# Moving four of layer 1's modulation vectors between layer 0's output columns, an earlier score pair, and weight blocks that wait for their own rows

## What is computed

```
for i in range(DEPTH):                                   # DEPTH = 2
    mod = silu_c @ ada_w[i] + ada_b[i]
    mod_c = silu_cc @ ada_w[i] + ada_b[i]
    sh1, sc1, g1, sh2, sc2, g2 = jnp.split(mod[:, None, :], 6, axis=-1)
    h_lat = modulate(rmsnorm(x, norm1_g[i]), sh1, sc1)    # h_ctx alike
    y_lat, y_ctx = even_mixer(...) if i % 2 == 0 else odd_mixer(...)
    x = x + g1 * y_lat
    h2 = modulate(rmsnorm(x, norm2_g[i]), sh2, sc2)
    out = peer(tokens, p_w_q[i], p_keys1[i], p_keys2[i], p_u[i], p_v[i])
    x = x + g2 * out
return rmsnorm(x, final_g)
```

## Time and profile before

| | before |
|---|---|
| median of 3 runs | 2415.6 us (2414.28 to 2417.3) |
| the profiled execution's own time | 2415.03 us |
| its span | 2413.2 us |
| PE, DVE, ACT, POOL busy | 57%, 64%, 15%, 62% |
| moved by DMA | 936.90 MB, mean 388 GB/s |
| queue of the gathers | 84.1% of 16 engines' span |
| queue of SP (weights) | 129.78 MB, 14.6% |

### The profile page before, as it was taken

The page is one execution under the profiler, slowest core; times in us unless marked ns, Lnnn a source line. Parts: engine busy times, 40 slices in busy tenths (PEclk is TensorE's granted clock), DMA queues, the critical chain, the costliest instruction groups (busy, mean ns, idle before and its releaser), DMA issues.

```text
span 2413.2 us, 21643 instructions
## 1 busy us (share of the span) xinstructions
PE 1386.2 (57%) x6926; PEld 621.5 (26%) x6926; DVE 1542.4 (64%) x4025; ACT 360.2 (15%) x731; POOL 1490.2 (62%) x1546
## 2 busy tenths in 40 slices
PE   6997774456674655335443556648866565334333
PEld 2456421123331433001100112315533133001000
DVE  1338578878955665777766655623898646777543
ACT  1421201112301110110100101202222011000000
POOL 0004576677677666767777767630577776777772
PEclk9999886668797877567655766879987787665567
DMA  9967899999999999999999999989999999999997
GB/s 367 346 220 302 323 406 407 409 409 409 382 406 408 405 407 407 410 409 409 409 409 409 405 409 409 406 326 379 353 409 396 404 407 407 409 409 409 410 409 302
DMA packets 286799, 936.90 MB, mean 388 GB/s; under 512 B 27728, under 2 KB 28512, under 8 KB 286432
## 3 DMA queue, kind: packets, MB, share of 16 engines
q0 software_dynamic: 221184, 805.40, 84.1%
q1 hardware_dynamic: 64704, 129.78, 14.6%
q10 hardware_dynamic: 800, 0.34, 0.1%
HBM read 934.36 MB, written 1.05 MB: 388 GB/s over the span
## 4 chain that ended last, share of the span: by engine, by line
DMA 35%; POOL 23%; PE 17%; DVE 12%; issue 10%; ACT 2%; SPq 1%; POOLq 0%; DVEq 0%; ACTq 0%
DMA RING<-in_p_v,IDV 19%; POOL RING L879 16%; DMA RING<-in_p_u,IDX 10%; PE acc L1552 5%; DVE RING L960 4%; POOL WR L879 3%; PE wk L1801 2%; PE wk L1627 2%; PE wk L1841 2%; DMA BC<-in_p_v,IDV 2%; POOL H L879 2%; DMA X<-in_p_v,IDV 2%; POOL BC L879 2%; POOL X L879 1%; PE wk L1583 1%
## 5 line engine op out<-in xcount | busy, mean ns | idle before, releaser
L1552 PE MATMUL acc<-RING,ST 128*32 128x512 f32 x2044 | 569.8, 919 | 522.6 <-DMA RING<-in_p_v,IDV 411.6
L960 DVE SCALAR_TENSOR_TENSOR RING<-RING,acc 128x1024 f32<-128x1024 f32 x576 | 687.4, 1219 | 277.7 <-DMA RING<-in_p_u,IDX 258.6
L879 POOL DMA_INDIRECT RING<-in_p_u,IDX x576 | 558.7, 970 | 412.9 <-DVE IDX L1279 192.6
L879 POOL DMA_INDIRECT RING<-in_p_v,IDV x511 | 496.8, 972 | 218.6 <-issue 144.9
L1552 PEld LDWEIGHTS acc<-RING,ST 128*32 128x32 f32 x2044 | 104.5, 144 | 750.4 <-issue 743.0
L1552 PE MATMUL acc<-WR,ST 128*32 128x512 f32 x428 | 158.7, 935 | 63.8 <-DMA BC<-in_p_v,IDV 53.2
L1552 PE MATMUL acc<-X,ST 128*32 128x512 f32 x288 | 114.4, 911 | 92.3 <-DMA RING<-in_p_v,IDV 92.3
L879 POOL DMA_INDIRECT H<-in_p_u,IDX x82 | 78.9, 962 | 123.5 <-DVE IDX L1279 96.7
L960 DVE SCALAR_TENSOR_TENSOR H<-H,acc 128x1024 f32<-128x1024 f32 x82 | 100.0, 1220 | 81.6 <-DMA H<-in_p_u,IDX 80.3
L879 POOL DMA_INDIRECT WR<-in_p_v,IDV x107 | 101.0, 944 | 32.6 <-issue 31.4
L1552 PE MATMUL acc<-BC,ST 128*32 128x512 f32 x148 | 76.7, 958 | 72.9 <-DMA RING<-in_p_v,IDV 72.9
(11 more groups left out here) (277 smaller groups left out, 2469.7 us busy)
## 6 DMA issues: line engine op xcount, KB each, us to landing
RING<-in_ada_w SPq DMA_DIRECT2D x30, 1024.0 KB, 12.3
WR<-in_p_w_q SPq DMA_DIRECT2D x20, 1024.0 KB, 12.5
WR<-in_ada_w SPq DMA_DIRECT2D x15, 1024.0 KB, 12.8
RING<-in_p_u,IDX POOLq DMA_INDIRECT x576, 17.6
WR<-in_o_w_in SPq DMA_DIRECT2D x9, 1024.0 KB
WR<-in_e_w_in SPq DMA_DIRECT2D x8, 1024.0 KB, 15.0
RING<-in_p_v,IDV POOLq DMA_INDIRECT x511, 18.2
RING<-in_p_w_q SPq DMA_DIRECT2D x7, 1024.0 KB, 6.9
```

Source lines behind the costliest of these rows:

```text
L879: pool.indirect_dma_start(out=row_at(row), out_offset=None, in_=tables[kind], in_offset=bass.IndirectOffsetOnAxis(ap=rows, axis=0)).then_i ...
L960: nc.vector.scalar_tensor_tensor(out=row_at(row), in0=row_at(row), scalar=1.0, in1=acc[:, 1, :], op0=ALU.mult, op1=ALU.mult, accum_out=A[: ...
L1552: ins = nc.tensor.matmul(acc[32 * g:32 * g + 32, 0, hf * 512:hf * 512 + 512], ST[:, c % 2, s, :], row_at(rows[g][0])[:, hf * 512:hf * 512 ...
```

## The change

Three things. In `front0`, layer 1's `ada` 6 (with `adaT`, `adaD`) now stands around layer 0's second output column, and its `ada` 8 behind that column; both leave `front1`. In `fills0`, the context tokens' last score item, heads 6 and 7, stands at fill 2 and not 3. In `block_slots` (moved below `gather_rows`, since it now reads `ROWS`) the ring slots are taken between the layers in the order in which their rows are summed, a block waits for the last sum of its own two rows (`last_sum`) and not for all 512, and the first-layer slots 3, 4, 5 are open to fewer blocks.

```
-    s += [("out", 0, first, 0), ("outD", 0, first, 0), ("out", 0, first, 1), ("ada", 0, 10, 2), ("outD", 0, first, 1), ...
+    s += [("out", 0, first, 0), ("outD", 0, first, 0), ("ada", 1, 6, 2), ("out", 0, first, 1), ("adaT", 1, 6, 2), ("adaD", 1, 6, 2), ("ada", 1, 8, 2), ("adaT", 1, 8, 2), ("adaD", 1, 8, 2), ("ada", 0, 10, 2), ("outD", 0, first, 1), ...
...
-        put(f, 3, ("score", 0, ctx, (6, 7)))
+        put(f, 2, ("score", 0, ctx, (6, 7)))
...
-    s += [("restA", 0), ..., ("restE", 1), ("ada", 1, 6, 2),
+    s += [("restA", 0), ..., ("restE", 1),
...
-    s += [("out", 1, first, 0), ("adaT", 1, 6, 2), ("outD", 1, first, 0), ("out", 1, first, 1), ("adaD", 1, 6, 2), ("outD", 1, first, 1),
-          ("normA", 1, 2, 0), ("ada", 1, 8, 2), ("normB", 1, 2, 0), ("hT", 1, 2, first), ("adaT", 1, 8, 2), ("adaD", 1, 8, 2)]
+    s += [("out", 1, first, 0), ("outD", 1, first, 0), ("out", 1, first, 1), ("outD", 1, first, 1),
+          ("normA", 1, 2, 0), ("normB", 1, 2, 0), ("hT", 1, 2, first)]
...
+def last_sum(slot):
+    rows = [("x", 2), ("x", 3)] if slot == YSLOT else [("ring", 2 * RSLOTS.index(slot) + i) for i in range(2)]
+    return max([i + 1 for i in range(32 * TOPK) if ROWS["v", i][0] in rows])
...
-    idle.update({s: (AT["experts_end", 0], s) for s in (*RSLOTS, YSLOT)})
+    idle.update({s: (AT["experts_end", 0], last_sum(s) - 32 * TOPK) for s in (*RSLOTS, YSLOT)})
...
-            free += EARLY_DOTS if last < dots[0] else ()
+            free += EARLY_DOTS if last < AT["topk", 0, 2, (1,), 0] else ()
...
-                elif slot in RSLOTS[:4]:
-                    sp.wait_ge(dotted, 32 * TOPK)
-                    if any(...):
-                        sp.wait_ge(vsum, 32 * TOPK)
                 elif slot in RSLOTS or slot == YSLOT:
-                    sp.wait_ge(vsum, 32 * TOPK)
+                    if slot in RSLOTS[:4]:
+                        sp.wait_ge(dotted, 32 * TOPK)
+                    sp.wait_ge(vsum, last_sum(slot))
```

More of the change, by code:

```diff
@@ L177, in front0 @@
                                                7: [("adaT", 1, 0, 2)], 8: [("adaD", 1, 0, 2)]})
-    s += [("out", 0, first, 0), ("outD", 0, first, 0), ("out", 0, first, 1), ("ada", 0, 10, 2), ("outD", 0, first, 1), *[("normA", 0, 2, t) for t in first],
+    s += [("out", 0, first, 0), ("outD", 0, first, 0), ("ada", 1, 6, 2), ("out", 0, first, 1), ("adaT", 1, 6, 2), ("adaD", 1, 6, 2), ("ada", 1, 8, 2), ("adaT", 1, 8, 2), ("adaD", 1, 8, 2), ("ada", 0, 10, 2), ("outD", 0, first, 1), *[("normA", 0, 2, t) for t in first],
           *[("normB", 0, 2, t) for t in first], ("adaT", 0, 10, 2), ("ada", 1, 2, 1), ("adaD", 0, 10, 2),
@@ L522, with block_slots, row_slot @@
 ROWS, LAST_IN = gather_rows()
+def last_sum(slot):
+    rows = [("x", 2), ("x", 3)] if slot == YSLOT else [("ring", 2 * RSLOTS.index(slot) + i) for i in range(2)]
+    return max([i + 1 for i in range(32 * TOPK) if ROWS["v", i][0] in rows])
+def block_slots():
+    early = next(i for i, name in enumerate(BLOCKS) if name[0] == "score")
+    end = AT[KV1]
+    sums = [AT["experts", l, ORDER[l][0], 1, 0] for l in range(DEPTH)]
+    dots = [AT["experts", l, ORDER[l][0], 0, 0] for l in range(DEPTH)]
+    slots, users, idle = [], {}, {s: (-1, s) for s in (*range(WSLOTS), XSLOT)}
+    idle.update({s: (AT["experts_end", 0], last_sum(s) - 32 * TOPK) for s in (*RSLOTS, YSLOT)})
+    idle[ZSLOT] = (AT["restY", 1], ZSLOT)
+    for i, name in enumerate(BLOCKS):
+        at, last = AT[name[:-1]], AT[LAST_USE.get(name[:-1], name[:-1])]
+        if i < early:
+            slot = i % (WSLOTS + len(EARLY_ROWS))
+        else:
+            free = [*range(WSLOTS if last < sums[0] or at >= end else 2)] + [XSLOT] * (at >= end)
+            free += EARLY_DOTS if last < AT["topk", 0, 2, (1,), 0] else ()
+            free += EARLY_SUMS if last < sums[0] else ()
+            free += RSLOTS[:4] if AT["experts_end", 0] < at and last < dots[1] and name[:3] != ("ada", 1, 10) else ()
+            free += RSLOTS[4:] if AT["experts_end", 0] < at and last < sums[1] else ()
+            free += [YSLOT] if AT["experts_end", 0] < at and last < AT["experts", 1, 0, 1, 2] else []
+            free += [ZSLOT] if AT["restY", 1] < at and last < AT["attA", 1, LAT, 8] else []
+            slot = min(free, key=lambda s: idle[s] if s != 2 or at < end else max(idle[s], (end, -1)))
+        idle[slot] = (last, i)
+        u = users.setdefault(slot, [])
+        slots.append((slot, len(u) + 1, u[-1] if u else None))
+        u.append(name)
+    return slots
+def row_slot(l, r):
+    return next((s for s in ((WSLOTS + EARLY_ROWS.index(x) for x in EARLY_ROWS if x <= r < x + 2) if l == 0 else
+                             (RSLOTS[r // 2],))), None)
+SLOTS = block_slots()
 class Count:
```

3 lines of the change are left out of this document (1 added, 2 removed).

## The result

| | before | changed |
|---|---|---|
| median of 21 runs each | 2416.71 us (2413.26 to 2417.64) | 2419.5 us (2417.24 to 2429.03) |
| the profiled execution, its span | 2415.03, 2413.2 us | 2418.27, 2416.5 us |
| moved by DMA, mean | 936.90 MB, 388 GB/s | 936.90 MB, 388 GB/s |

The ratio is 1.0016 with a 95% interval of 1.001 to 1.0022: a loss of 2.8 us, inside the 0.2% that the prediction called no change. Forecast were 2418.5 us and a difference of +3.5 us; the spans differ by +3.3.

The account below looks back on a forecast made before the run. DMA transfers were taken as the floor, 2291 of the 2413 us span, the rest being DMA idle time. The terms summed as 10.0 - 10.5 - 3.7 + 7.7 = +3.5, so 2418.5 us, range 2410 to 2427.

Parts of the forecast that it names:

- A: Layer 0's output stage: both `ada` items there lengthen PE's work and delay the first gather, +10.0 us.
- B: Layer 0's first quarters: heads 6 and 7 one quarter earlier shorten the second DMA hole, -10.5 us, ends -7.6 and -13.0.
- The rival in which the hole stays open: Layer 0's second hole: later gelu and rows 12 and 13 hold POOL nearly as long; gain only 3, 2426 us; chance 0.10.
- C: Between the layers: without the two `ada` items layer 1's first gather goes out sooner, -3.7 us, ends -1.9 and -5.5.
- D: After layer 1's first gather: three blocks miss the idle hole and lengthen that stretch, +7.7 us, ends 0 and +8.1.
- The first rival: Layer 1's start: DVE sets the pace, so the three late blocks are free; 2408 to 2411 us; chance 0.22.
- E: Between the layers: blocks waiting only for their own rows' sums go out earlier and win nothing, 0 us, ends 0 and +8.
- The rival in which early blocks hold the last gathers: End of layer 0: early blocks delay a lagging DMA engine's last gathers, +6 taken, up to +8; 2424.5 us; chance 0.12.
- one sign of being wrong: End of layer 0: prediction wrong if the last sums come over 20 us behind the last gather's issue.
- a rival at 2421.3: Layer 1's first scores: PE, idle longer, runs the next score at a slow clock too, C loses 2.8 us; chance 0.08.

Follow-up runs that it names:

- the control: The changed kernel measured once more, unedited, on a chip with the usual times: 2418.67 us, ratio 1.0015 to before.
- the kernels with the rule: Layer 1's second input column blocks barred from slots of ring rows 10 to 15: changed kernel 2421.73 us; with both `ada` items back 2409.67 us.
- the score alone: The kernel before with only the score item of heads 6 and 7 at fill 2, not 3: 2401.69 us, ratio 0.9944.
- the pair with the rule: Changed kernel, second input column blocks barred from ring rows 10 to 15: 2421.73 us; the same with `ada` 10 ahead of layer 1's scores: 2407.18 us.
- The kernel with the rule: The changed kernel with layer 1's second input column blocks barred from the slots of ring rows 10 to 15: 2421.73 us, ratio 1.0026.
- e4_sums_again: The changed kernel with blocks between the layers waiting for all 512 sums again, as before the change: 2419.49 us, ratio 1.0014.
- The changed order with `ada` 10 early: Changed kernel with `ada` 10 ahead of layer 1's scores: 2418.28 us; with second input column blocks also barred from ring rows 10 to 15: 2407.18 us.

## Why the prediction was right

**A, +10.0: measured +10.1.** The stretch to the first gather grew from 195.0 to 205.1 (204.9 in the control; 206.4 to 208.1 in the four other kernels that begin alike, so the size is known to some 3 us). The wait for ACT's copy stands twice, as counted. The kernels with the rule confirm it without the rest: 196.4 with the items back, 206.4 with them moved.

**B, -10.5: measured -12.3, and -13.1 when done alone.** The mechanism came as worked out. The first gelu was put at 243.4 and A's 10 us later, 253.4: it starts at 253.43. The gather of the earlier trace rows at 267.14 was put at 259.5 plus the same shift, 269.5: it goes out at 269.77. Mis-sized was the reserve of 2.5 us for a thin queue. The upper end of 13.0, all the idle time of the hole, was nearly reached by the change and fully by the score alone, which has shares of 0.98 to 1.03 through it. Its median fell by 14.8, the span of the profiled execution by 13.4; the interval on the ratio (about 10 to 18 us) holds both. The rival in which the hole stays open fell.

**C, -3.7: measured -4.2.** The copies of `hT` no longer wait for the scale: from PE's start on the last sums to its first score are 56.1 us, for 59.1, so 3.0 of the 3.7 came as worked out. The rest is that the first score took 5.33 us and not 6.45, at a granted clock of 0.69 and not 0.57, where the rival had feared a worse one. The control has 3.6 for the whole of C, so that rest is within the scatter.

**D, +7.7: measured +8.7.** SP stopped where I said, with 17 blocks issued as forecast, until 1701 (about 1702). That late blocks lengthen the stretch by their bytes is shown by the pair with the rule: letting SP past `ada` 10 takes 11.4 us off the last stretch, of which the bytes make an estimated 9.6. In the changed kernel itself the stretch carries 285.9 MB (723.7 us at 395 GB/s) for 283.1 before (715.0 at 396), which is about three blocks. In the prediction's words the blocks "lengthen" a stretch at share 1.02, and that was only the half of it. The changed kernel also lets PE wait for the blocks (0.99 us ahead of 1728.21), and POOL for PE (6.00 and 6.87 us). That these waits cost nothing of their own rests on the windows, which stay at 1.02. The kernel with the rule, where both are gone, gained nothing, but another wait came in their place. The first rival, in which DVE paces the stretch and the blocks are free, fell.

**E, 0: measured +1.0 once, -0.4 in the control, and the median with the old waits is the same.** The rival in which early blocks hold the last gathers, with its +6 to +8, did not come. But one sign of being wrong did: last sums over 20 us behind the last gather's issue (20.5 in the profiled execution, 19.1 in the control). The scatter of that stretch is as large as the sign's margin, so it told nothing. The rival was also tried on less than I had worked out. I had nine blocks out by 1616; SP's timeline has six (1601.69 to 1615.94), each issue after the third taking 2.4 to 6.4 us. Between the last gather's issue and the last sums 7.2 MB moved (354 GB/s), 6.6 in the control, for 5.4 before: one to two blocks more, and not six. What six would do is open.

And 0 was right for a smaller question than I had asked. I had read from the diff when blocks are issued, and only for one block which slot it takes. Without the moved items the new slots and waits cost 16.5 us, half of it by one block. In the changed kernel that cost does not show: late blocks keep the DMA engines busy while POOL waits (1.04 in the windows of 10 us from 1730 to 1750). So the result is better told by adding the parts in order: the score pair -14.8 us, the new slots and waits +16.5, the moved items on top of these +0.5. My sum had -10.5 and +14 for the score and the moved items, and it met the result because A, C, D and the covered slots are what the complete change shows. I had not foreseen that the two costs would cover each other; in this the total met the result by luck. With the misplaced blocks out of the way, moving the items costs 12.1 us (2409.67 to 2421.73), which is what A, C and D say in sum (14.0) within 2 us.

The best kernel found is the one-line change, 2401.69 us. It beats before by 14.8 and the changed kernel by 17.0 us on the same chip.

## What to carry to other kernels

Measure a change's parts alone before a compound one is judged: here a gain of 14.8 us lay under a loss of the same size. When weights borrow the buffers of a gather ring, choose the slot by which row the first gathers will want, not only by which row comes free first; an in-order queue makes one such block a stall for all behind it. And filling one idle stretch of the DMA engines is worth nothing where the transfers come out of another idle stretch, whose length an engine's chain sets.

## What the runs showed of the hardware

**The clock can make a tail.** Of 72 executions of before on the chips with the usual times, none was above 2418.72 us. The changed kernel has 2429.03 and 2426.97 among its 31, the changed kernel with the rule 2428.40 and 2426.83 among 11, and e4_sums_again 2431.02 and 2424.90 among 12. The changed order with `ada` 10 early has none in 15 executions (at most 2419.53), and the kernels with the two `ada` items between the layers none in 24 (at most 2421.22). That of 2431.02 was profiled. These are three windows between the layers, first of the changed kernel, then of that execution:

```profile
1640.00:1650.00 10.00, 8.22 (x61) 7.40 (x57) 9.52 (x22) 4.75 (x9) 0.00 (x0) 0.96 0.76 265
1650.00:1660.00 10.00, 9.09 (x41) 5.37 (x40) 3.13 (x5) 2.48 (x3) 0.00 (x0) 1.00 0.48 160
1660.00:1670.00 10.00, 7.86 (x19) 3.20 (x17) 3.29 (x5) 0.00 (x0) 0.00 (x0) 1.00 0.19 75
```
```profile
1640.00:1650.00 10.00, 9.20 (x56) 8.03 (x56) 6.97 (x13) 3.98 (x7) 0.00 (x0) 0.69 1.05 387
1650.00:1660.00 10.00, 8.28 (x44) 7.88 (x44) 5.85 (x13) 2.66 (x7) 0.00 (x0) 0.65 0.97 358
1660.00:1670.00 10.00, 9.44 (x18) 4.51 (x19) 0.51 (x1) 2.47 (x3) 0.00 (x0) 0.67 0.42 134
```

The granted clock (the third number from the end) is 0.65 to 0.69, a mix of the levels 1.2 and 2.4 GHz, where it was 0.96 to 1.00. Ahead of it both had PE idle for more than half of the time: in the window at 1610 it was busy 4.75 of 10 us in the changed kernel and 3.64 in the other, at 0.50 and 0.60. The one was back near full speed by 1640, the other was not. But before was busy 3.64 there as well, at 0.67, and had 1.00 in the window at 1640; what decides between the two is not shown. The first gather of layer 1 comes 82.7 us behind the last sums, for 73.9, and the same 276 matmuls of that stretch kept PE busy 68.00 us, for 58.54. The Trainium skill, TensorE: Matmul & The Clock Gate, Part 1, has activity release the throttled state; the windows agree in kind. That the other five have the same cause is not shown, since they have no profile: their mean granted clocks are 0.736 to 0.739, at the low end, but another execution of e4_sums_again had 0.735 and took 2419.59. In the prediction this was a rival at 2421.3; it is no shift of the median but a few executions some 5 to 12 us longer.

**One chip moved less, and unevenly.** The same kernel before took 2685.79 us on it, 11% more than elsewhere. The GB/s line of the kernel with the score alone, there:

```profile
GB/s 369 361 163 317 364 404 375 357 364 307 309 342 395 315 353 346 369 366 361 369 333 373 365 408 366 286 334 384 338 366 319 370 402 355 353 390 334 363 384 311
```

Slices 6 to 25, which lie within layer 0's gathers, go from 307 to 408 where the earlier trace rows has 382 once and otherwise 405 to 410: the rate comes and goes. The Trainium skill, HBM Reference, section Specifications (TRN2), gives some 358 GB/s for a core while its pair streams as well, and well above that alone. That another program drew on the same memory would fit, and no run here can show it. Differences of a few us can't be read on such a chip: the intervals were roughly two to three times as wide there.
